# ScalarE rounds queries and keys and builds the diagonals; GpSimd keeps the low halves and splits a second output chunk early

## The chip, the cores and the metric

The program runs on 1 core of a Trainium2 chip. The metric is device time in microseconds (us) of one execution. The core has five engines that run beside each other and are tied only by semaphores: TensorE (PE in the profile: matmuls; PEld: its weight loads), VectorE (DVE), ScalarE (ACT), GpSimd (POOL) and SyncE (SP), which here only starts DMAs. Each engine runs its own instructions strictly in order, so a wait in one instruction holds up everything behind it on that engine.

## What is computed

Four layers on a 512 x 1024 fp32 stream: two layers of kind A (sliding-window attention SWA with 6 heads, a pooling mixer, causal latent attention MLA with 6 heads, then a gated MLP), one of kind R (a gated linear recurrence beside cross-attention XA with 4 heads over 256 memory rows) and one of kind F (causal "forgetting" attention FOX with 8 heads beside XA with 4), the last two with a squared-ReLU MLP.

```python
for l in range(DEPTH):                       # kind A, twice
    proj = rms_norm(x, attn_norm[l]) @ w_in[l]
    q_a, k_a, v_a, u_b, cq_c, ckv_c, kr_c = jnp.split(proj, split_idx, axis=-1)
    mixed = concat([swa_mixer(q_a, k_a, v_a, ...), pool_mixer(u_b, ...), mla_mixer(cq_c, ckv_c, ...)])
    x = x + mixed @ w_out[l]
    h = rms_norm(x, ffn_norm[l])
    x = x + (jax.nn.silu(h @ w_gate[l]) * (h @ w_up[l])) @ w_down[l]
for layer in range(DEPTH):                   # kind R, then kind F
    h = rms_norm_2(x, norm_mix[layer])
    y_mix, xq = rglru_group(h, ...) if layer == 0 else fox_group(h, ...)
    y_mem = memory_group(xq, mem, ...)       # XA: softmax(rms(q) rms(k)^T / sqrt(128)) v
    x = x + concat([y_mix, y_mem]) @ w_out[layer]
    x = x + sqrelu_mlp(rms_norm_2(x, norm_mlp[layer]), w_mlp_in[layer], w_mlp_out[layer])
```

Every attention head is softmax(q k^T) v with normalized q and k.

## The kernel before

**Precision.** TensorE works on fp32r, a rounded fp32. To keep fp32 accuracy an operand is held as a high half (the value rounded to fp32r) and a low half (the rest), and each product takes three passes: high x high, high x low, low x high (lines 807 to 816, by the helper `passes`).

**Weights.** They stream from HBM in chunks of 16 blocks of 128 x 128 (1 MB) into two slots `raw0`, `raw1`. GpSimd splits a chunk into `wh` and `wl` (`split`, lines 612 to 638): it waits until the chunk has landed, then (line 618) until TensorE has begun the chunk before it (`w_used`), which shows that the slot's old content is used up; then two TENSOR_SCALAR of 128 x 1024 (L627) and four TENSOR_TENSOR of 128 x 512 (L633). TensorE takes 48 matmuls for a chunk.

**One attention stage**, in the order of the work for head hd (units: the query tiles, of one or two heads):
- VectorE `prep` (line 1962) scales a unit's query and key tiles into `t[:, 0]`, `t[:, 1]` and signals `norm_qk`.
- GpSimd `prep` (line 709) rounds them to `qh`, `kh` (L669) and signals `hi_ready`; then forms `ql`, `kl` (L665) and signals `qk_ready`. From the third unit on it first waits until the scores of the unit before have released the slot (line 714).
- TensorE `score_rows` (line 1094): q x k of the high halves, query rows on the partitions, in two halves (two row blocks each) into banks 0 and 1. It waits for `hi_ready` at a unit's start.
- VectorE `maxima` (line 2026): TENSOR_REDUCE of the row maxima (L2034, L2041, L2043, L2045) into `mx`; for SWA also the maximum with the sink (L1651); then two TENSOR_SCALAR (L2052), one for each row block, that write -max times the identity into `dg`. After the second half `dg_ready`.
- TensorE `score_columns` (line 1124) waits for `dg_ready`, and at a unit's start for `qk_ready`; keys on the partitions: three passes, then `ones_r` x `dg` (L1150), which subtracts each query's maximum; masks or biases. Banks 2 and 3.
- ScalarE `exponentials` (line 1512) writes `pt`; TensorE `weighted` (lines 1172, 1182, 1187) multiplies with the values into bank 4; ScalarE `reciprocal` (line 1534, two activations of `rt`); VectorE `out` (line 2057) multiplies into `sq`, which has two buffers, so it first waits until GpSimd has consumed the output two before; GpSimd `mixed` (L669 and L705) rounds and splits it into `act`. `weighted` of the next head waits until bank 4 is emptied by `out`.

TensorE, VectorE, ScalarE and GpSimd each go through the heads in a fixed order: TensorE score_rows(hd+1) first half, score_columns(hd), score_rows(hd+1) second half, weighted(hd-1); VectorE maxima(hd+1) first half, prep, out(hd-2), maxima(hd+1) second half, and in layer R one step of the recurrence (`recurrence`, line 1888); ScalarE reciprocal(hd-2), exponentials(hd); GpSimd prep, at one head (`chunk_at`: 3 in SWA, 3 in XA of layer R, 5 in FOX) the split of the first of the four chunks of the output projection, then mixed(hd-2).

**Output projection.** `out_proj` (line 1222) uses the four chunks one after the other, two banks each; the first needs the mixed tiles one by one, the second waits for its split and for VectorE's `resid` (line 2102), which adds the first two banks to x (L1647, x<-x,ps). Chunks 2 to 4 of this projection are split after the attention (line 769). In layer 0 VectorE runs `decay_rates` (line 1742, about 30 instructions on 128 x 4 elements) between the last `out` and `resid`.

## Time and profile before

| | us |
|---|---|
| median of 3 runs | 2573.95 (2565.67 to 2575.25) |
| the profiled execution | 2568.36 |
| its span in the trace | 2566.6 |
| mean granted clock of TensorE | 0.964 of full speed |

| engine | busy us | share of the span | instructions |
|---|---|---|---|
| PE | 2391.1 | 93% | 10786 |
| DVE | 1204.1 | 47% | 1482 |
| ACT | 406.3 | 16% | 688 |
| POOL | 1723.7 | 67% | 1432 |

Busy time is the time in which an engine had an instruction of its own under way; the shares say who could be the limit on average, not who is the limit in a stage. The stages with attention are at 100 to 265 us (layer 0), 755 to 908 (layer 1), 1440 to 1502 (layer 2, kind R) and 2045 to 2168 (layer 3, kind F); the rest is projections and MLPs.

### The profile page before, as it was taken

How to read it: one execution, taken by the hardware profiler on the slowest of the kernel's cores; microseconds unless marked ns; L12 is line 12 of the kernel's file. 1: busy time of each engine (PE TensorE's matmuls, PEld its weight loads, DVE VectorE, ACT ScalarE, POOL GpSimd, SP SyncE). 2: the span in 40 equal slices, each digit the busy share in tenths (PEclk: the TensorE clock that was granted, in tenths of full speed). 3: DMA queues.
4: the chain of work that ended last, by engine and by line, in shares of the span. 5: the costliest groups of instructions: out<-in, count | busy, mean ns of one | idle time of the engine just before them, and what ended most of it. 6: DMA issues, size and time to landing. Idle time of an engine off the chain costs nothing. (4 is left out here: it accounts for less than half of the span.)

```text
span 2566.6 us, 29137 instructions
## 1 busy us (share of the span) xinstructions
PE 2391.1 (93%) x10786; PEld 1922.9 (75%) x10786; DVE 1204.1 (47%) x1482; ACT 406.3 (16%) x688; POOL 1723.7 (67%) x1432
## 2 busy tenths in 40 slices
PE   5978899999997899999998789999999898999999
PEld 4666688888866678888886558888887675888887
DVE  7776543332378644332248655315345463550340
ACT  3122111110122311111011411001111132110000
POOL 5565677777756577777776577767765655786774
PEclk9988999999998899999999789999999988999999
DMA  4210122223321012222232112222232200222222
GB/s 141 91 38 1 66 98 98 98 73 101 113 67 53 1 67 98 98 98 84 96 118 79 50 66 91 101 90 95 99 115 82 83 17 2 97 98 99 98 98 82
DMA packets 37841, 207.89 MB, mean 81 GB/s; under 512 B 3532, under 2 KB 10316, under 8 KB 16888
## 3 DMA queue, kind: packets, MB, share of 16 engines
q1 hardware_dynamic: 37752, 206.70, 23.2%
q8 instruction: 56, 0.92, 0.1%
q14 instruction: 33, 0.27, 0.0%
HBM read 204.55 MB, written 2.13 MB: 81 GB/s over the span
## 5 line engine op out<-in xcount | busy, mean ns | idle before, releaser
L633 POOL TENSOR_TENSOR wl<-raw,wh 128x512 fp32r<-128x512 f32 (+1 forms) x776 | 1051.8, 1387 | 0.0
L627 POOL TENSOR_SCALAR wh<-raw 128x1024 fp32r<-128x1024 f32 (+1 forms) x388 | 430.7, 1130 | 593.4 <-PE ps L811 447.7
L811 PE MATMUL ps<-h,wh 128*128 128x512 f32 x1576 | 618.6, 392 | 27.9 <-POOL wl L633 9.2
L815 PE MATMUL ps<-h,wh 128*128 128x512 f32 x1576 | 614.4, 390 | 0.0
L816 PE MATMUL ps<-h,wl 128*128 128x512 f32 x1576 | 614.4, 390 | 0.0
L811 PE MATMUL ps<-act,wh 128*128 128x512 f32 x1120 | 438.3, 391 | 7.4 <-DVE x L1647 5.6
L815 PE MATMUL ps<-act,wh 128*128 128x512 f32 x1120 | 436.5, 390 | 0.0
L816 PE MATMUL ps<-act,wl 128*128 128x512 f32 x1120 | 436.3, 390 | 0.0
L811 PEld LDWEIGHTS ps<-h,wh 128*128 128x128 f32 x1576 | 296.5, 188 | 100.1 <-issue 29.4
L816 PEld LDWEIGHTS ps<-h,wl 128*128 128x128 f32 x1576 | 296.4, 188 | 62.2
L815 PEld LDWEIGHTS ps<-h,wh 128*128 128x128 f32 x1576 | 296.7, 188 | 61.8 <-issue 1.0
L1647 DVE TENSOR_TENSOR x<-x,ps 128x512 f32<-128x512 f32 x80 | 55.0, 688 | 483.8 <-PE ps L816 483.3
L811 PEld LDWEIGHTS ps<-act,wh 128*128 128x128 f32 x1120 | 210.8, 188 | 53.4 <-issue 6.6
L816 PEld LDWEIGHTS ps<-act,wl 128*128 128x128 f32 x1120 | 210.7, 188 | 44.1
L815 PEld LDWEIGHTS ps<-act,wh 128*128 128x128 f32 x1120 | 210.8, 188 | 43.9 <-issue 0.5
L1647 DVE TENSOR_TENSOR t<-ps,rstd 128x512 f32<-128x512 f32 x108 | 74.7, 692 | 105.5 <-PE ps L816 104.4
L1647 DVE TENSOR_TENSOR nt<-ps,rstd 128x512 f32<-128x512 f32 x44 | 30.4, 692 | 192.9 <-PE ps L816 192.7
L1647 DVE TENSOR_TENSOR ssq<-ssq,sq 128x512 f32<-128x512 f32 (+1 forms) x80 | 81.0, 1013 | 78.9 <-ACT sq L1320 78.1
L1320 ACT ACTIVATE h<-x,vec 128x512 fp32r<-128x512 f32 x64 | 46.3, 724 | 449.3 <-DVE x L1647 438.5
L1320 ACT ACTIVATE act<-t 128x512 f32 (+1 forms) x64 | 40.5, 633 | 462.7 <-DVE t L1655 462.7
L1647 DVE TENSOR_TENSOR act<-t,act 128x512 f32 (+1 forms) x64 | 69.0, 1077 | 63.6 <-ACT act L1320 63.6
L669 POOL TENSOR_SCALAR qh<-t 128x512 fp32r<-128x512 f32 (+1 forms) x30 | 18.5, 617 | 119.3 <-DVEq L1994 50.5
(339 smaller groups left out, 2896.4 us busy)
## 6 DMA issues: line engine op xcount, KB each, us to landing
raw<-w_gu SPq DMA_DIRECT2D x44, 1024.0 KB, 4.8
raw<-w_up SPq DMA_DIRECT2D x32, 1024.0 KB, 4.8
raw<-w_down_b SPq DMA_DIRECT2D x32, 1024.0 KB, 4.8
raw<-w_down_a SPq DMA_DIRECT2D x32, 704.0 KB, 4.0
raw<-w_in_a SPq DMA_DIRECT2D x14, 1024.0 KB, 4.8
raw<-w_in_f SPq DMA_DIRECT2D x13, 1024.0 KB, 4.9
raw<-w_in_r SPq DMA_DIRECT2D x11, 1024.0 KB, 4.9
raw<-w_out_a SPq DMA_DIRECT2D x8, 1024.0 KB, 7.8
```

Of the source, the lines that this page charges most:

```text
L627: pool.tensor_scalar(hi_s[:, part], raw[s][:, part], 1.0, 1.0, ALU.mult, ALU.mult).then_inc(hi_done, 1)
L633: ins = pool.tensor_tensor(lo_s[:, part], raw[s][:, part], hi_s[:, part].bitcast(F32), ALU.subtract)
L669: pool.tensor_scalar(out, in0, scale, 1.0, ALU.mult, ALU.mult).then_inc(hi_done, 1)
L811: first = pe.matmul(out, w_hi, v_hi, start=start, stop=False)
L815: pe.matmul(out, w_hi, v_lo, start=False, stop=False)
L816: return pe.matmul(out, w_lo, v_hi, start=False, stop=stop)
L1320: return sc.activation(out, in_, f, **kw)
L1647: dve.tensor_tensor(out, in0, in1, op).then_inc(sig.sem, 1)
```

## The change

1. Rounding queries and keys moves from GpSimd to ScalarE: ScalarE gets a `prep` of its own, which waits for `norm_qk` (and for the slot), writes `qh` and `kh` with ACT.Copy and signals `hi_ready`. GpSimd's `prep` waits for `hi_ready` and writes only the low halves.
2. The diagonals move from VectorE to ScalarE (`diagonals`): an activation of the identity with the maximum as its scale. The sign goes into the ones (`neg_ones_r`). `mx` gets a second buffer. VectorE keeps the reduces, and for SWA the maximum with the sink, which signals `max_ready`.
3. ScalarE's order for head hd becomes reciprocal(hd-2), diagonals(hd+1) first half, exponentials(hd), prep, diagonals(hd+1) second half.
4. GpSimd splits two output chunks within the attention. The first is at SWA head 3 as before, at XA head 2 in layer R (was 3) and at FOX head 4 (was 5). The second is at MLA head 3, XA head 4 in layer R and FOX head 7; in place of `w_used` it waits for the last filling of the bank that the slot's old chunk fed (`slot_done`). After the attention two chunks are left instead of three.

```diff
+            def split(s, nblk, first=False, slot_done=None):
...
-                if not first:
+                if slot_done is not None:
+                    pool.wait_ge(ready[slot_done], bk.filled(slot_done, -1))
+                elif not first:
                     pool.wait_ge(w_used, used.at())
...
-            def prep(m, u, after=None):
-
-
-                pool.wait_ge(norm_qk, nqk.up())
-                if after is not None:
...
+            def prep(m, u):
+
+
+                pool.wait_ge(hi_ready, qkh.up())
                 s, sk = m.slot(u), m.kslot(u)
...
-                tsc(qh[s][q, :], t[q, 0, :])
-                for r, (k_hi, k_lo) in zip(parts, keys):
-                    tsc(k_hi[r, 0:n], t[r, 1, 0:n])
-                pool.sem_inc(hi_ready, 1)
                 tt(ql[s][q, :], t[q, 0, :], qh[s][q, :].bitcast(F32), ALU.subtract)
...
                     if hd == chunk_at:
 
                         split_all(1, BLOCKS)
+                    if hd == second_at:
+
+                        split_all(1, BLOCKS, slot_done)
...
-                    attention(MLA)
+                    attention(MLA, second_at=3, slot_done=7)
...
-                    attention(XA, None, 3, True)
+                    attention(XA, None, 2, True, second_at=4, slot_done=3)
...
-                    attention(FOX, XA, 5)
+                    attention(FOX, XA, 4, second_at=7, slot_done=0)
                     attention(XA)
-                split_all(n_out - 1, nblk)
+                split_all(n_out - 2, nblk)
...
+            def prep(m, u, after=None):
+
+
+                sc.wait_ge(norm_qk, nqk.up())
+                if after is not None:
+                    sc.wait_ge(ready[3], bk.filled(3, (2 * after + 1) if m.kind == "causal" else after))
+                q, n = m.qrows(), m.nkeys()
+                last = fn(qh[m.slot(u)][q, :], t[q, 0, :], ACT.Copy)
+                for r, (k_hi, k_lo) in key_parts(m, u):
+                    last = fn(k_hi[r, 0:n], t[r, 1, 0:n], ACT.Copy)
+                last.then_inc(hi_ready, 1)
...
+                    for i in (0, 1) if half == 0 else (2, 3):
+                        ins = fn(dgs[m.name][hd % 2][:, i, :], ident[:, :], ACT.Copy, scale=mx[hd % 2][:, i:i + 1])
+                    if half:
+                        ins.then_inc(dg_ready, 1)
+
+                diagonals(0, 0)
+                prep(m, 1)
+                diagonals(0, 1)
                 for hd in range(m.heads + 2):
                     if hd >= 2:
                         reciprocal(hd - 2)
+                    if hd + 1 < m.heads:
+                        diagonals(hd + 1, 0)
                     if hd < m.heads:
                         exponentials(hd)
+                    if m.starts(hd):
+                        prep(m, m.starts(hd), hd)
+                    if hd == m.heads and nxt:
+                        prep(nxt, 0)
+                    if hd + 1 < m.heads:
+                        diagonals(hd + 1, 1)
...
-                    for i in two:
-                        ins = dve.tensor_scalar(dg[:, i, :], ident[:, :], mx[:, i:i + 1], -1.0, ALU.mult, ALU.mult)
-                        if i == TB - 1:
-                            ins.then_inc(dg_ready, 1)
-                            dgr.up()
```

How it stands on the engines. GpSimd in layer 0, MLA heads 2 to 4 (`act<-sq` is mixed, `qh`, `kh`, `ql`, `kl` are prep), before:

```order
L669 TENSOR_SCALAR act<-sq 64x512
L705 TENSOR_TENSOR act<-sq,act 64x512
L669 TENSOR_SCALAR qh_79<-t 96x512
L669 TENSOR_SCALAR kh_83<-t 64x512
L665 TENSOR_TENSOR ql_81<-t,qh_79 96x512
L665 TENSOR_TENSOR kl_85<-t,kh_83 64x512
L669 TENSOR_SCALAR act<-sq 64x512
```

And now, at the same place:

```order
L722 TENSOR_TENSOR act<-sq,act 64x512
L682 TENSOR_TENSOR ql_81<-t,qh_79 96x512
L682 TENSOR_TENSOR kl_85<-t,kh_83 64x512
L644 TENSOR_SCALAR wh_54<-raw_52 128x1024 x2
L650 TENSOR_TENSOR wl_56<-raw_52,wh_54 128x512 x4
L686 TENSOR_SCALAR act<-sq 64x512
```

The two roundings are gone, and the second output chunk stands between the last prep and the mixing of MLA's second head.

GpSimd in layer R, XA heads 1 to 5, before (each `act<-sq` pair is one mixed; after the one of the recurrence at head 1 came head 2's two, then the split):

```order
L665 TENSOR_TENSOR kl_85<-t,kh_83 128x256
L669 TENSOR_SCALAR act<-sq 128x512
L705 TENSOR_TENSOR act<-sq,act 128x512
...
L627 TENSOR_SCALAR wh_55<-raw_53 128x1024 x2
L633 TENSOR_TENSOR wl_57<-raw_53,wh_55 128x512 x4
```

And now:

```order
L682 TENSOR_TENSOR kl_85<-t,kh_83 128x256
L686 TENSOR_SCALAR act<-sq 128x512
L722 TENSOR_TENSOR act<-sq,act 128x512
L644 TENSOR_SCALAR wh_55<-raw_53 128x1024 x2
L650 TENSOR_TENSOR wl_57<-raw_53,wh_55 128x512 x4
...
L644 TENSOR_SCALAR wh_54<-raw_52 128x1024 x2
L650 TENSOR_TENSOR wl_56<-raw_52,wh_54 128x512 x4
```

The first split has moved ahead of head 2's two outputs; four outputs lie between it and the second split, two behind that.

ScalarE in SWA of layer 0, from the reciprocal of one head on (`rt` reciprocal, `pt` and `es` exponentials), before:

```order
L1320 ACTIVATE rt<-es 64x512
L1320 ACTIVATE rt<-rt 64x512
L1320 ACTIVATE pt_a<-ps 128x512
L1320 ACTIVATE pt_a<-ps 128x384
L1320 ACTIVATE es<-ps,vec 64x512
```

And now:

```order
L1333 ACTIVATE rt<-es 64x512
L1333 ACTIVATE rt<-rt 64x512
L1333 ACTIVATE dg_96<-ident,sm 128x128 x2
L1333 ACTIVATE pt_a<-ps 128x512
L1333 ACTIVATE pt_a<-ps 128x384
L1333 ACTIVATE es<-ps,vec 64x512
L1333 ACTIVATE dg_96<-ident,sm 128x128 x2
```

The exponentials of a head now stand behind the first two diagonals of the next head and ahead of the last two.

## Rows read from the trace of the kernel before

**Rows 1.** Busy time by stretch: start:end length, busy us of each engine, clock, DMA.
```profile
400.00:450.00 50.00, 50.00 (x223) 41.39 (x222) 19.27 (x19) 5.72 (x9) 35.43 (x28) 1.00 0.29 105
128.00:203.00 75.00, 54.59 (x322) 45.21 (x321) 58.71 (x99) 19.43 (x33) 41.99 (x43) 0.87 0.09 34
203.00:262.00 59.00, 51.23 (x238) 38.82 (x237) 34.85 (x65) 17.82 (x36) 37.96 (x40) 0.88 0.00 1
1440.00:1502.00 62.00, 39.79 (x122) 23.59 (x122) 42.31 (x55) 9.98 (x17) 34.10 (x33) 0.72 0.07 27
```

**Rows 2.** Waits of PE over the span: waiter, awaited, us in total, times, longest.
```profile
PE ps L1187 <- DVE sq L1647: 17.8, 5, 10.0
PE ps L1120 <- POOLq L723: 13.0, 6, 4.9
PE ps L811 <- DVE x L1647: 11.6, 7, 5.6
PE ps L1146 <- DVE dg L2052: 8.1, 4, 4.1
PE ps L1182 <- DVE sq L1647: 7.9, 6, 2.5
PE ps L1104 <- POOLq L723: 7.9, 4, 3.2
PE ps L1146 <- DVE dg_swa L2052: 4.9, 5, 1.2
```

**Rows 3.** Groups by form: shapes, count, busy us, mean ns, idle before.
```profile
L2052 DVE TENSOR_SCALAR dg<-ident,sm 128x128 fp32r<-128x128 f32 x136 | 67.4, 537 | 5.3
L1320 ACT ACTIVATE pt<-ps 128x128 f32<-128x128 f32 x6 | 1.7, 277 | 1.7 <-PE ps L1152 1.7
L1320 ACT ACTIVATE pt<-ps,nck 128x128 f32<-128x128 f32 x4 | 1.5, 368 | 1.0 <-PE ps L1152 1.0
L1320 ACT ACTIVATE act<-t 128x512 f32 x48 | 30.4, 633 | 221.4 <-DVE t L1655 221.4
L669 POOL TENSOR_SCALAR qh<-t 128x512 fp32r<-128x512 f32 x18 | 11.1, 619 | 82.1 <-DVEq L1994 39.2 <-PE ps L1152 15.8 <-PE ps L1155 14.0
L705 POOL TENSOR_TENSOR act<-sq,act 64x512 fp32r<-64x512 f32 x32 | 40.7, 1271 | 2.7
```

**Rows 4.** Order of time, layer 0's output projection, DVE, then POOL, then PE.
```profile
270.25 1.21 DVE L1647 TENSOR_TENSOR sm<-sm 128x4 f32<-128x4 f32 x1
274.37 0.17 DVE L1651 TENSOR_SCALAR sm<-sm 128x4 f32<-128x4 f32 x1
278.03 0.69 DVE L1647 TENSOR_TENSOR x<-x,ps 128x512 f32<-128x512 f32 x1
...
268.89 5.02 POOL L633 TENSOR_TENSOR wl<-raw,wh 128x512 fp32r<-128x512 f32 x4
...
278.86 0.77 PE L811 MATMUL ps<-act,wh 128*128 128x512 f32 x1 [5.58 <-DVE x L1647]
```

**Rows 5.** Order of time, layer 1, SWA head 3, DVE.
```profile
817.49 2.52 DVE L2052 TENSOR_SCALAR dg<-ident,sm 128x128 fp32r<-128x128 f32 x2
```

**Rows 6.** Order of time, layer 1, MLA's last heads, ACT, DVE, POOL, PE.
```profile
885.79 0.28 ACT L1320 ACTIVATE pt_a<-ps 128x128 f32<-128x128 f32 x1 [0.31 <-PE ps L1152]
...
896.53 0.69 DVE L1647 TENSOR_TENSOR sq<-ps,rt 64x512 f32<-64x512 f32 x1 [1.92 <-issue]
...
888.83 1.29 POOL L665 TENSOR_TENSOR kl<-t,kh 64x512 fp32r<-64x512 f32 x1
...
902.81 3.84 PE L1172 MATMUL ps<-pt_a,vom 128*128 128x512 f32 x8 [2.12 <-DVE sq L1647]
```

**Rows 7.** Order of time, layer R, XA's last heads, POOL, DVE, PE.
```profile
1485.54 6.72 POOL L633 TENSOR_TENSOR wl<-raw,wh 128x512 fp32r<-128x512 f32 x4
...
1494.44 0.69 DVE L1647 TENSOR_TENSOR sq<-ps,rt 128x512 f32<-128x512 f32 x1 [4.52 <-POOL act L705]
...
1495.18 3.78 PE L1187 MATMUL ps<-pt0b,rxv 128*128 128x512 f32 x4 [9.96 <-DVE sq L1647]
```

More of the change, by code:

```diff
@@ L224, in half, with qrows, nkeys @@
         return h % 2 if self.per_unit == 2 else 0
+    def qrows(self):
+        return slice(0, 96) if self.name == "mla" else slice(0, P)
+    def nkeys(self):
+        return M_MEM if self.name == "xa" else T
     def vrow(self, h):
@@ L306, in build @@
         anti_r = keep("anti_r", [P], F32R)
-        ones_r = keep("ones_r", [P], F32R)
+        neg_ones_r = keep("neg_ones_r", [P], F32R)
         maskt_r = keep("maskt_r", [P], F32R)
@@ L337, in build, with key_parts @@
         key_tiles = {"swa": swa_k, "mla": one_k, "fox": fox_k, "xa": one_k}
+        def key_parts(m, u):
+            if m.name == "swa" and u:
+                return []
+            keys = key_tiles[m.name][m.kslot(u)]
+            rows = slice(0, 64) if m.name == "mla" else slice(0, P)
+            return zip([rows] if len(keys) < 2 else [slice(0, 64), slice(64, P)], keys)
         pt0 = view("pt0", H_AT + 16384, [4 * T])
@@ L638, in split @@
                 split_out.up()
-            nqk = Count(norm_qk, kept)
+            qkh = Count(hi_ready, kept)
             mixo = Count(mix_out, kept)
@@ L1149, in score_columns @@
                         maxima = dg[:, q0 // P:(q0 + n) // P, :].rearrange("p b n -> p (b n)")
-                        last = pe.matmul(out, ones_r[:, :], maxima, start=False, stop=m.kind == "full")
+                        last = pe.matmul(out, neg_ones_r[:, :], maxima, start=False, stop=m.kind == "full")
                         if m.kind == "causal":
@@ L1420, in in_a @@
                     fn(kraw[:, i, :], ps[tt % 4][:, :], ACT.Copy).then_inc(free[tt % 4], 1)
+                prep(SWA, 0)
                 for i in range(MLA_HEADS):
@@ L1503, in in_f @@
                 stat(6, 1, full, 2, 1.0 / D)
+                prep(FOX, 0)
                 for i in range(4):
@@ L1509, in in_f, with attention @@
                 bk.close(USES_IN_F)
-            def attention(m, l):
+            def attention(m, l, nxt=None):
                 def exponentials(hd):
@@ L1546, in reciprocal, with diagonals @@
                     fn(rt[v, :], rt[v, :], ACT.Exp, scale=-1.0).then_inc(recip_ready, 1)
+                def diagonals(hd, half):
+                    if m.name == "swa":
+                        sc.wait_ge(max_ready, mxr.up())
+                    elif m.kind == "causal":
+                        sc.wait_ge(free[0], bk.emptied(0, 2 * hd + half))
+                        sc.wait_ge(free[1], bk.emptied(1, 2 * hd + half))
+                    else:
+                        sc.wait_ge(free[half], bk.emptied(half, hd))
+                    for i in (0, 1) if half == 0 else (2, 3):
[5 more added lines that the diff above has]
+                diagonals(0, 1)
                 for hd in range(m.heads + 2):
@@ L1582, in _ @@
                     in_a()
-                    attention(SWA, l)
+                    attention(SWA, l, MLA)
                     attention(MLA, l)
@@ L1594, in _ @@
                         in_f()
-                        attention(FOX, l)
+                        attention(FOX, l, XA)
                     attention(XA, l)
@@ new lines, in maxima @@
+                        return
+                    b = half
+                    dve.wait_ge(ready[b], bk.filled(b, hd))
+                    if m.kind == "band" and b == 0:
+                        dve.tensor_reduce(mxs[:, 0:1], ps[0][:, P:256], AX_X, ALU.max).then_inc(dve_step, 1)
+                        dve.wait_ge(dve_step, chain.up())
+                        dve.tensor_reduce(mxs[:, 1:2], ps[0][:, 256:T], AX_X, ALU.max).then_inc(free[0], 1)
+                    else:
+                        dve.tensor_reduce(mxs[:, 2 * b:2 * b + 2], ps[b][:, :].rearrange("p (a c) -> p a c", a=2),
+                                          AX_X, ALU.max).then_inc(free[b], 1)
```

59 lines of the change are left out of this document (23 added, 36 removed).

## The prediction

> **What bounds the kernel now.** I read the stages first, then who waits for whom, then the order of time at the places that wait. In a stretch of the MLP TensorE is busy for all of its 50 us at full clock [rows 1]: nothing of the change lies there, and such stretches are some four fifths of the span. In the attention stretches TensorE is not full: in 128 to 203 us it works 54.6 of 75, in 203 to 262 it works 51.2 of 59, in 1440 to 1502 only 39.8 of 62, at a mean clock of 0.87, 0.88 and 0.72 [rows 1]. VectorE is the busiest of the others there (58.7 of 75), ScalarE the idlest (19.4 of 75, 10.0 of 62). So what can be won is idle time of TensorE in the attention, and of it what these waits hold [rows 2]: for the diagonals 8.1 + 4.9 us; for the output buffer `sq`, through bank 4, 7.9 us in SWA and 17.8 in XA; for `hi_ready` 7.9 + 13.0 us; and for the first add to x, 11.6, of which 5.6 once, in layer 0. These 71 us are the ceiling, apart from the clock: it is at the 1.2 GHz level in parts of these stretches.
>
> **Part 1: the diagonals leave VectorE.** The 136 instructions (two for each half of a head, 68 pairs) cost 67.4 us there, 537 ns each on average [rows 3]. A pair takes from 0.5 us up to 2.52 us, the latter while GpSimd splits a chunk [rows 5]. On ScalarE an activation of the same size takes 277 ns, with a per-partition operand 368 [rows 3]; those read PSUM, these read SBUF. I take 0.65 us a pair (bounds 0.55 and 0.8), 44 us for the 68 pairs, beside TensorE's work except at the handoffs.
> The row behind this: a VectorE instruction on 128x2 or 128x4 elements in SBUF takes 0.17 us alone and 1.21 while GpSimd is splitting [rows 4]. The Trainium skill ("SBUF — State Buffer", section "Who interferes with whom") says that the port pair which VectorE and GpSimd share is locked for a whole instruction and that ScalarE never waits for it; the trace agrees on the VectorE side, and for ScalarE no pair of such rows exists yet. By that page's rule the diagonals would cost the same beside a split.
> In SWA the chain is: VectorE reduces, out(hd-2) with ScalarE's two reciprocal steps between, reduce, diagonal; each weighted() and score_columns() waits on it, 7.9 and 4.9 us in both layers together [rows 2]. With 0.5 to 2.5 us per head off VectorE I expect the heads without a split to become TensorE-bound and the one with a split to keep about 1 us. ScalarE's chain there, reciprocal 1.26 (two of 0.633 [rows 3]), diagonals 0.65, exponentials about 1.8, diagonals 0.65, ends just about when TensorE has done weighted(hd-1). Gain: 12.8 less 5 that stays, or 8 us for the two layers. The waits of 8.1 us at the first heads (4.1 at most) shrink little, since only two pairs lie on that chain, by 0.5 each: 1 us is in the 8.
>
> **Part 2: rounding on ScalarE.** GpSimd takes 619 ns a tile [rows 3] and comes late where it is mixing outputs (a mixed is 0.62 + 1.27 us [rows 3]); ScalarE takes 633 ns for a copy of that size from SBUF [rows 3], so the move itself is neutral and the gain is the queue ahead of it. At the second unit of MLA and of both XA stages TensorE waits up to 3.2 and 4.9 us for it [rows 2]. GpSimd's mixed goes from that path, 1 us in each A layer, 1.3 in layer F, 0.5 at the start in R. Where GpSimd only waited for the slot, ScalarE has to finish the exponentials first and nothing changes; in F's second such place I count +0.3. Sum: 2 us in the A layers, 2 in F with 0.5 for the chunk and the FOX start. What hides the copies in the steady state: in MLA head 3 the last exponential ends at 886.07 [rows 6]; copies 1.24, diagonals 0.65 give 888.0, and the next score_columns starts at 888.9. The cover is 0.9 us. If it is gone, each head pays the excess.
>
> **Part 3: the second chunk early.** In the projection itself it is worth little in layers 1, R and F: the second chunk was ready 0.3 to 0.5 us after the bank that it also waits for, so 0.3 us each. Its price is 7.1 us of GpSimd time (2.1 + 5.0 [rows 4]), up to 9.4 beside a busy VectorE (2.7 + 6.7, its second part in [rows 7]). In MLA: low halves end about 890.0 (before 890.12 [rows 6]), the split 897.2, mixed(1) 899.1. VectorE's out(3), at 896.53 before [rows 6], must wait for that mixed since `sq` has two buffers: 2.6 us later, weighted(4) 1.5 us later, and with it the rest, since GpSimd has mixed(2) only at 901.1. Cost +1.5 in each A layer, and +0.25 where the diagonals delay the first exponential: 3.2 us for both, net of 0.3. At FOX head 7 GpSimd has room, no cost.
> In layer 0 it takes something else away. The split at 266.9 to 273.9 [rows 4] runs beside `decay_rates`, whose tiny instructions then take 1.2 us instead of 0.17 [rows 4]; so the add to x comes at 278.03 and TensorE stands for 5.58 us [rows 4]. With the chunk already split GpSimd is idle there: some 30 instructions at 0.2 us end before TensorE has done the first chunk, the gap falls to the 1.0 us of the add, and 4.6 us go. After that gap TensorE ran at 1.2 GHz for a while (the first matmul 0.77 us against 0.39): another 1.2. Together 5.8.
>
> **Part 4: layer R.** Before, the split sat between the recurrence step of head 2 and output 1. VectorE waited for GpSimd's mixed until 1494.44, and TensorE stood 9.96 us [rows 7]. Now the first split starts as soon as the recurrence output of head 1 is mixed, about 3 us earlier than the old order would reach that point since VectorE is 5 us of diagonals lighter: 1470 to 1479.4 at the contended 9.4. Output 0 and recurrence 2 are then mixed by 1483.3; output 1 leaves VectorE at 1482.1 (0.6 us later than now), recurrence 3 at 1487.2, output 2 at 1490.5 where it was 1495.1. The last weighted() follows at once, at half or full clock (3.8 or 2.0 us [rows 7] for its first part), and the projection starts 4.6 to 7 us earlier. The second split (1489 to 1496) makes output 2's mixed late, 1498.4, but the projection's first chunk needs it only at its seventh block, 4 us in. I take 5.5.
>
> **The sum.** 2568.4 - 8 (SWA) - 2 (A layers' rounding) + 3.2 (MLA's end) - 5.8 (layer 0's projection) - 5.5 (R) - 2 (F) = 2548.3, a change of -20 us or 0.8%. The profiled execution lies 5.6 us below the median of the three runs; the same change from the median is 2554. I give 2553.
>
> **The rivals.**
> A. As worked out, -14 to -27 us.
> B. More: the shorter gaps also keep the clock at 2.4 GHz through the starts of SWA, MLA and XA, where a stretch of layer R shows 0.72 and SWA 0.87 [rows 1]. If a third of the time lost to the low clock there (about 30 us in all, from 0.13 x 75 in one SWA, as much in the other, and 0.28 x 62 less the idle part) comes back: -30, 2543. Against it: the 5 us waits at the two starts of MLA, on VectorE, are untouched.
> C. ScalarE's order takes part of the gain: the exponentials stand behind diagonals that wait for VectorE's reduce, and VectorE stands in out() until GpSimd has mixed. If the diagonals cost 0.8 a pair and SWA keeps 1 us a head more (10 heads), with R at 4: about -8, 2566. Both splits contended at 9.4 us give the same, +2.3 at each MLA end.
> D. Slower: ScalarE becomes the bound. Place: diagonals(hd+1) second half, behind exponentials and copies, in MLA and FOX. The cover is 0.9 us where I could read it; the 12 heads of MLA, 8 of FOX and 12 of SWA would each have to exceed it by 1.1 us, +35 against -20, which gives +15 and 2589. It decides from 0.63 us a head on (20 us over 32 heads). Against it: ScalarE works 5.7 us in 50 outside and 19.4 in 75 here [rows 1], and the added 44 us + 30 units of copies fit.
> The Trainium skill ("VectorE: DVE Perf Modes", section on the TRN2 errata) speaks on D's side: a ScalarE instruction that reads SBUF pays a fixed 224 cycles, so many small ones are dear. An estimate from its figures for 128 elements at 1.2 GHz is 0.29 us each, 0.59 a pair; by it the sum would be some 1 us better than mine, and no row here shows an SBUF read of 128 columns on ScalarE.
> E. The change doesn't do what it says: the second split waits, since its chunk has not landed or the bank's count is met late. Then the projection finds it late as now, layer 0's 5.8 is lost and the A layers gain less: -12, 2562.
>
> **How the numbers follow.** A 0.45, B 0.15, C 0.22, D 0.09, E 0.09. A measurement of this kernel can tell about 0.5%, 13 us, from no change. A (but for its edge) and B are faster by more, C and E are within, D is slower: faster 0.60, same 0.31, slower 0.09. The range takes in A, C, E and most of B, with 5 us for the spread of the runs: 2535 to 2570.
>
> **What would show it.** In the new profile: the wait of L811 for the add to x has lost its 5.6; `sm` instructions of 128x4 all near 0.17; diagonals on ScalarE in pairs of 0.6 to 0.7, also during splits; the waits for diagonals in SWA near zero; in MLA's last two heads a wait for `sq` of 3 to 4 us where it was 2.1; in R no wait near 10 us, but one of about 6 before output 1. I am wrong if TensorE waits for ScalarE's diagonals in the middle of MLA or FOX (D), if a pair takes over 0.8 (C), or if the stretches 1440 on show the higher clock (B).

## The result, and the profile after

The changed kernel takes 2547.35 us (median of 4 runs, 2546.21 to 2551.81), the kernel before beside it 2574.56 (2565.67 to 2575.25). The ratio is 0.9905, 95% interval 0.9881 to 0.993: faster by about 1%. The prediction was 2553 us with a range of 2535 to 2570. The profiled execution took 2546.21 us (span 2544.4) where that of before took 2568.36. All medians and ratios below are of fast runs; one run of r_both came in a slower state, at 3440.56 us and a mean granted clock of 0.65, and is left out.

The page of the changed kernel, span and busy time of the engines. VectorE lost 76 us of work, ScalarE gained 84, GpSimd lost 36. TensorE was busy 2385.7 us where it was busy 2391.1 with the same matmuls, so of the 22.2 us by which the span is shorter 16.8 are idle time and 5.4 are a higher granted clock:

```profile
span 2544.4 us, 29116 instructions
PE 2385.7 (94%) x10786; PEld 1918.6 (75%) x10786; DVE 1128.1 (44%) x1322; ACT 490.2 (19%) x910; POOL 1687.4 (66%) x1370
```

Waits of TensorE over the span, changed kernel (waiter, awaited, us in total, times, longest), beside [rows 2]:

```profile
PE ps L1198 <- DVE sq L1699: 14.2, 5, 6.2
PE ps L1183 <- DVE sq L1699: 11.9, 5, 3.7
PE ps L1131 <- ACT kh L1333: 9.4, 4, 4.0
PE ps L1157 <- ACT dg_swa L1333: 7.2, 6, 1.9
PE ps L822 <- DVE x L1699: 7.1, 10, 1.1
PE ps L1115 <- ACT kh L1333: 4.8, 4, 1.6
PE ps L1157 <- ACT dg L1333: 4.2, 6, 1.7
PE ps L822 <- POOL act L722: 1.9, 1, 1.9
PE ps L1193 <- DVE sq L1699: 0.5, 2, 0.3
```

Line numbers have moved: L1198 was L1187 (weighted, XA), L1183 was L1172 (MLA), L1193 was L1182 (SWA), L1157 was L1146 (diagonals), L1131 and L1115 were L1120 and L1104 (rounded halves), L822 was L811. The sum of the seven lines of [rows 2] was 71.2 us; what answers to them is 47.4. MLA's end (L1183) is not among the seven: it was 5.7 before and is 11.9 now. SWA's wait for bank 4 went from 7.9 to 0.5, but its wait for the diagonals rose from 4.9 to 7.2. The 1.9 for `act` is a wait of layer R's projection, read below. The longest single waits, 10.0 in layer R and 5.6 at the first add to x, are 6.2 and 1.1 now.

Groups by form: the diagonals and the roundings on ScalarE, and one pair of diagonals in layer 0 while GpSimd splits (171.2 to 176.2), in order of time:

```profile
L1333 ACT ACTIVATE dg<-ident,sm 128x128 fp32r<-128x128 f32 x136 | 47.0, 393 | 50.3 <-DVE sm L2085 22.0 <-DVE sm L2094 16.2 <-DVE sm L2099 11.9
L1333 ACT ACTIVATE qh<-t 128x512 fp32r<-128x512 f32 x18 | 11.3, 626 | 16.7 <-DVEq L2046 16.6
...
172.20 0.70 ACT L1333 ACTIVATE dg<-ident,sm 128x128 fp32r<-128x128 f32 x2
```

One diagonal takes 393 ns, and a pair 0.69 to 0.70 us since the two overlap. A pair beside a split takes the same 0.70, where VectorE's took 2.52 [rows 5]. The 67.4 us of [rows 3] became 47.0.

**A ledger by stage.** Where the time went can be read closely, since both kernels run the same VectorE instructions in the same order at the ends of the stages. I take their start times as marks: the first reduce of a stage, SWA's sum of head 4 (es<-ps,es), MLA's out(2) and out(5), the last out of layers R and F, and the last add to x of a projection. The first column starts at the last add of layer 0's attention projection, so it holds layer 0's MLP too. An entry is how much longer or shorter a kernel takes from mark to mark than the kernel before (us, profiled executions; two values are layers 0 and 1).

| | to SWA start, layer 1 | SWA | MLA to out(2) | out(2) to out(5) | projection, layer 0 | R | projection, R | F |
|---|---|---|---|---|---|---|---|---|
| changed | +1.0 | -5.9, -5.4 | -1.9, -2.0 | +3.8, +4.1 | -7.0 | -8.2 | +3.3 | -4.4 |
| only_diag | +0.8 | -5.6, -6.2 | +2.4, -0.7 | -0.2, +0.8 | +0.8 | -6.9 | 0.0 | -5.6 |
| only_round | +1.0 | +1.3, +0.7 | -1.0, -1.0 | 0.0, +0.3 | -0.1 | -0.9 | 0.0 | -4.4 |
| undo_diag | +1.0 | +1.2, +0.7 | +1.5, -1.1 | +3.7, +3.9 | -7.0 | -3.4 | 0.0 | -3.4 |
| undo_round | 0.0 | -5.0, -4.6 | +1.5, +1.5 | +3.8, +5.1 | -7.0 | -7.0 | +3.3 | -4.3 |
| undo_second | +1.0 | -5.9, -5.5 | -2.0, -2.1 | +0.5, +0.7 | -0.1 | -6.9 | 0.0 | -1.4 |
| mla_count | +1.0 | -5.9, -5.4 | -1.9, -2.0 | +0.5, +0.8 | -7.0 | -8.2 | +3.4 | -4.5 |
| mla4 | +1.0 | -5.9, -6.3 | -2.0, -1.9 | +3.9, +4.5 | -7.0 | -6.5 | 0.0 | -4.0 |
| mla4_r4 | +1.0 | -5.9, -6.3 | -2.0, -1.9 | +0.5, +0.7 | -7.0 | -12.7 | +1.0 | -4.7 |
| r_both | -0.5 | -4.9, -6.5 | -2.0, -2.0 | -1.2, +0.7 | -6.3 | -8.2 | -0.5 | -4.0 |
| best2 | -0.8 | -4.1, -5.8 | -1.9, +0.2 | +0.5, -0.9 | -7.0 | -12.7 | 0.0 | -1.4 |
| decay_first | 0.0 | 0.0, 0.0 | 0.0, 0.0 | 0.0, +0.2 | -6.5 | -0.3 | 0.0 | -5.2 |

The rest (layer 0's start, 0.7 to 2.8 us later than in the kernel before, the MLPs, the other projections) adds 0.3 to 4.2 us. How far a single entry can be trusted is seen where the code is the same: SWA, MLA and the projections mostly repeat within 0.1 us, sometimes only within 2.5; layer R with its projection gave -4.9 and -6.5 for the same code (changed, mla4), and layer F -4.4, -4.5, -4.0, -4.7, -4.0 and -1.4 for one code, 0 and -5.2 for the other. The last is the clock, below. It has its part in other entries too: MLA to out(2) in only_diag is the same code in both layers and reads +2.4 at a mean granted clock of 0.75 (TensorE busy 46.6 us) and -0.7 at 0.84 (busy 42.0). SWA's gain in the changed kernel is free of it: TensorE is busy 40.3 and 40.2 us there where it was 39.7 and 41.2, and the idle time fell by 11.0 us in the two layers.

### The profile page after: what moved, and what is told of

Read it like the earlier page. It is cut to its first block, busy times and chain, and to the rows that moved or that the text cites. A ratio compares the mean times of both kernels' runs of the same rounds, so it can differ in the third digit from the quotient of the medians.

```text
span 2544.4 us, 29116 instructions
## 1 busy us (share of the span) xinstructions
PE 2385.7 (94%) x10786; PEld 1918.6 (75%) x10786; DVE 1128.1 (44%) x1322; ACT 490.2 (19%) x910; POOL 1687.4 (66%) x1370
## 4 chain that ended last, share of the span: by engine, by line
PE 57%; DVE 6%; POOL 2%; ACT 2%; issue 1%; DVEq 0%; POOLq 0%; ACTq 0%
PE ps L822 17%; PE ps L826 17%; PE ps L827 17%; POOL wl L650 1%; PE ps L1183 1%; PE ps L895 1%; PE ps L1157 1%; DVE nt L1707 1%; DVE uc L1707 1%; DVE nt L1699 1%; ACT rt L1333 1%; DVE t L1707 0%; POOL wh L644 0%; POOL act L722 0%; ACT nt L1333 0%
## 5 line engine op out<-in xcount | busy, mean ns | idle before, releaser
L822 PE MATMUL ps<-h,wh 128*128 128x512 f32 x1576 | 619.2, 393 | 28.1 <-POOL wl L650 9.4
L822 PE MATMUL ps<-act,wh 128*128 128x512 f32 x1120 | 437.8, 391 | 3.0 <-POOL act L722 1.9
L822 PEld LDWEIGHTS ps<-h,wh 128*128 128x128 f32 x1576 | 296.9, 188 | 100.2 <-issue 29.5
L822 PEld LDWEIGHTS ps<-act,wh 128*128 128x128 f32 x1120 | 210.7, 188 | 49.2 <-issue 3.1
L682 POOL TENSOR_TENSOR ql<-t,qh 128x512 fp32r<-128x512 f32 (+1 forms) x30 | 38.7, 1290 | 154.3 <-ACT kh L1333 75.9
```

Source lines behind the costliest of these rows:

```text
L682: pool.tensor_tensor(out, in0, in1, op).then_inc(hi_done, 1)
L822: first = pe.matmul(out, w_hi, v_hi, start=start, stop=False)
```

## The experiments

Each run was timed beside the kernel before, on the same chip, and its ratio is to that; the chips of different runs differ, so ratios compare better than medians.

### One part undone at a time: undo_diag, undo_round, undo_second

undo_diag, on VectorE in `maxima`, and the same two lines taken from ScalarE:

```diff
+                def diagonals(hd, half):
+                    for i in (0, 1) if half == 0 else (2, 3):
+                        ins = dve.tensor_scalar(dgs[m.name][hd % 2][:, i, :], ident[:, :],
+                                                mx[hd % 2][:, i:i + 1], 1.0, ALU.mult, ALU.mult)
+                    if half:
+                        ins.then_inc(dg_ready, 1)
```

> The changed kernel with the diagonals back on VectorE, directly behind its reduces (the minus stays in the ones, mx keeps its two buffers); rounding and the splits stay as changed. Theory 1, the parts act at separate places and add up: the 9.4 us that the two SWA stages gained go (the waits for the diagonals and for bank 4 come back there), about 1 us at each MLA start, and in layer R VectorE is again 5 us later at output 1, of which 2 to 3 us reach the end. Sum +12, about 2559 us. Theory 2, the SWA gain came mostly from rounding on ScalarE (GpSimd's roundings no longer stand before the mixed outputs): +3, about 2550, and the intervals between the sink sums of SWA stay at 6.0 to 7.0 us.

Measured: 2568.56 us (2564.0 to 2571.31), ratio to before 0.9984 (0.9973 to 0.9995). Without the diagonals nearly nothing of the gain is left, some 20 us less of it. That is more than either theory gave: SWA loses 7.1 and 6.1 us against the changed kernel and is slower than before, MLA's start loses 3.4 and 0.9, layer R with its projection 1.5. Theory 2 falls. Of theory 1 the places hold, the size doesn't. MLA's start in layer 0 is partly the clock: only_round, with the same code up to there, has -1.0 at a mean clock of 0.80 where undo_diag has +1.5 at 0.75.

undo_round, in GpSimd's `prep`, with ScalarE's `prep` removed:

```diff
+                pool.wait_ge(norm_qk, qkh.up())
+                if after is not None:
+                    pool.wait_ge(ready[3], bk.filled(3, (2 * after + 1) if m.kind == "causal" else after))
...
+                tsc(qh[s][q, :], t[q, 0, :])
+                for r, (k_hi, k_lo) in key_parts(m, u):
+                    tsc(k_hi[r, 0:n], t[r, 1, 0:n])
+                pool.sem_inc(hi_ready, 1)
```

> The changed kernel with the rounding back on GpSimd, ahead of its low halves; diagonals on ScalarE and the splits stay as changed. Theory 1: the second unit of MLA is late again (the wait for the rounded halves from 1.6 back to over 3 us), 2 us in each A layer; 1 to 2 us in layers R and F; MLA's end gets no better. Sum +5 to +7, about 2553 us. Theory 2, the rounding carries the SWA gain: +10 or more, about 2558, with the SWA intervals back near 8.5.

Measured: 2557.97 us (2553.93 to 2559.86), ratio 0.9934 (0.9915 to 0.9954). By the ledger the rounding is worth 3.4 us at each MLA start (-1.9 to +1.5, and -2.0 to +1.5), 0.8 to 0.9 in each SWA, and it costs 1.0 before each SWA. Of the 3.4 us 1.1 is idle time of TensorE (8.9 us for 7.9); the other 2.3 are the same matmuls at a mean clock of 0.75 for 0.80, and whether that comes with the change isn't shown. The SWA gain stays (theory 2 falls).

undo_second, four calls back to their old form:

```diff
-                    attention(MLA, second_at=3, slot_done=7)
+                    attention(MLA)
...
-                    attention(XA, None, 2, True, second_at=4, slot_done=3)
+                    attention(XA, None, 3, True)
...
-                    attention(FOX, XA, 4, second_at=7, slot_done=0)
+                    attention(FOX, XA, 5)
...
-                split_all(n_out - 2, nblk)
+                split_all(n_out - 1, nblk)
```

> The changed kernel with the splits as in the kernel before: one chunk early, at SWA head 3, XA head 3 and FOX head 5, none second. Theory 1: MLA's end loses its price, 3.8 us earlier in each A layer (7.6); layer 0's projection stands again for 5 to 6 us before the first add to x, and the starts of the projection's later chunks give back 1.5; layer R is back at its long wait before output 1, +4; layer F +1 to 2. Sum +4 to +6, about 2552 us. Theory 2, the second split costs more than it brings: below 2547.

Measured: 2549.21 us (2547.57 to 2551.11), ratio 0.9906 (0.9888 to 0.9925), against 0.9905 for the changed kernel. The entries come as theory 1 had them in the A layers: 3.3 us a layer back at MLA's end, 6.9 lost in layer 0's projection. Layer R with its projection is at -6.9 where the changed kernel is at -4.9, so moving the splits there brought nothing that shows. The early second chunk as a whole is worth nothing that can be measured: the ratios are equal, each within some 5 us.

### One part alone: only_diag, only_round

Both are the edits above put together: only_diag is undo_round with undo_second, only_round is undo_diag with undo_second.

> The kernel before with the diagonals alone on ScalarE (sign in the ones, mx with two buffers, ScalarE's order as changed); rounding on GpSimd and the splits as before. Theory 1, the diagonals carry nearly all: SWA 5 us earlier in each A layer, MLA's start 1.5 us later than before (its unit 1 still waits for GpSimd), layer R 5 to 7 us earlier, layer F 1 to 2: -12 to -14, about 2555 us where the kernel before has about 2568. Theory 2, the parts only work together: within 5 us of the kernel before.

> The kernel before with the rounding alone on ScalarE (GpSimd keeps the low halves); diagonals on VectorE and the splits as before. Theory 1: alone it gives nothing: 1 us lost at each SWA start (ScalarE rounds ahead of the squares that VectorE waits for), about 1 in each SWA, 0 to 1 won at the MLA starts: 0 to +4 us against the kernel before. Theory 2, as the prediction had it: 2 us won in the A layers and 1 to 2 elsewhere, -3.

Measured: only_diag 2549.79 us (2548.32 to 2553.35), ratio 0.9917 (0.99 to 0.9934); only_round 2567.26 (2565.11 to 2571.63), ratio 0.999 (0.9978 to 1.0002). The diagonals alone give nearly the whole gain, the rounding alone none that can be told from zero. Waits of TensorE in only_round:

```profile
PE ps L1193 <- DVE sq L1679: 7.3, 4, 2.4
PE ps L1115 <- ACT kh L1333: 6.3, 4, 2.5
```

With the diagonals on VectorE, SWA's wait for bank 4 is still there (7.3; 7.9 before), whoever rounds.

The two parts add up. By the whole times it is 0.83% for the diagonals and 0.10% for the rounding alone, and 0.94% for both (undo_second). At the MLA start the ledger seems to say otherwise (+2.4 and -0.7 for the diagonals, -1.0 twice for the rounding, -2.0 and -2.1 for both), but that is mostly the clock, as said above. The wait of TensorE for the second unit's rounded halves in layer 0 is read without it: 3.18 us before, 2.50 with the diagonals alone on ScalarE, 2.28 with the rounding alone, 1.64 with both. The kernel before, then the changed kernel:

```profile
211.00 0.47 PE L1104 MATMUL ps<-kh,qh 128*128 128x128 f32 x1 [3.18 <-POOLq L723]
204.82 0.48 PE L1115 MATMUL ps<-kh,qh 128*128 128x128 f32 x1 [1.64 <-ACT kh L1333]
```

The 1.0 us that rounding costs ahead of SWA can be read in the changed kernel, layer 0, order of time: ScalarE rounds the first unit before it takes the first square of the latent queries, and VectorE waits for that square. Before, the same instruction waited 1.17 us; in both layers the wait is 2.60 to 2.63 in every kernel traced that rounds there and 1.15 to 1.17 in every other one.

```profile
121.06 0.63 ACT L1333 ACTIVATE qh<-t 128x512 fp32r<-128x512 f32 x1 [2.25 <-DVEq L2046]
121.60 0.61 ACT L1333 ACTIVATE kh<-t 64x512 fp32r<-64x512 f32 x1
122.22 0.63 ACT L1333 ACTIVATE khb_swa<-t 64x512 fp32r<-64x512 f32 x1
122.87 0.59 ACT L1333 ACTIVATE sq<-ps 96x512 f32<-96x512 f32 x1
...
123.60 0.69 DVE L1699 TENSOR_TENSOR qc<-ps,cgq 96x512 f32<-96x512 f32 x1 [2.63 <-ACT sq L1333]
```

### MLA's end: mla_count, mla4

The changed kernel, layer 0, order of time: VectorE's out(3) and out(4) (sq<-ps,rt), GpSimd's mixing (act<-sq a head, act<-up a pooled tile), TensorE's weighted of heads 4 and 5:

```profile
248.24 0.69 DVE L1699 TENSOR_TENSOR sq<-ps,rt 64x512 f32<-64x512 f32 x1 [5.43 <-POOL act L722]
248.99 2.42 PE L1183 MATMUL ps<-pt,vom 128*128 128x512 f32 x8 [1.49 <-DVE sq L1699]
252.99 1.26 POOL L722 TENSOR_TENSOR act<-up,act 128x512 fp32r<-128x512 f32 x1
254.38 0.68 DVE L1699 TENSOR_TENSOR sq<-ps,rt 64x512 f32<-64x512 f32 x1 [5.44 <-POOL act L722]
255.12 4.12 PE L1183 MATMUL ps<-pt_a,vom 128*128 128x512 f32 x8 [3.70 <-DVE sq L1699]
```

out(4) starts right behind the pooled tile (252.99 + 1.26 = 254.25), not behind mixed(2), which is all that its buffer needs. VectorE's count of the mixed outputs is raised by two for the pooled tiles before out(4), though GpSimd mixes them after head 3. In the kernel before it cost nothing: out(4) at 257.50 was released by the reciprocal, the pooled tile was done at 256.90.

```diff
-                    if m.name == "mla" and hd == m.heads:
-
-                        mixs.n += 2
                     if hd >= 2:
                         out(hd - 2)
+                    if m.name == "mla" and hd == m.heads + 1:
+
+                        mixs.n += 2
```

> The changed kernel with one bookkeeping line of VectorE moved: the two pooled outputs that GpSimd mixes between MLA's outputs 3 and 4 are counted behind out(5) instead of before out(4), so that out(4) waits for mixed(2) and no longer also for the first pooled tile. Theory 1: in the changed kernel out(4) at 254.38 was released by the pooled tile at 254.25 while its reciprocal was there at 252.71; it now goes 1.5 to 1.7 us earlier in both A layers, about 3 us in all, 2544 us; the 1.5 us wait before it (out(3) for mixed(1), behind the split) stays. Theory 2, the chain through mixed(2) and the reciprocal ends at the same time: no change, 2547.

Measured: 2540.88 us (2539.44 to 2550.41), ratio 0.9885 (0.986 to 0.9911). The profiled executions differ by 6.8 us in all, twice what I expected. The same stretch in mla_count:

```profile
248.14 0.69 DVE L1699 TENSOR_TENSOR sq<-ps,rt 64x512 f32<-64x512 f32 x1 [5.43 <-POOL act L722]
252.69 0.68 DVE L1699 TENSOR_TENSOR sq<-ps,rt 64x512 f32<-64x512 f32 x1 [3.86 <-ACT rt L1333]
253.43 2.42 PE L1183 MATMUL ps<-pt_a,vom 128*128 128x512 f32 x8 [2.12 <-DVE sq L1699]
257.24 0.69 DVE L1699 TENSOR_TENSOR sq<-ps,rt 64x512 f32<-64x512 f32 x1 [3.86 <-ACT rt L1333]
```

out(4) comes 1.7 us earlier, as expected, and the eight matmuls behind it take 2.42 us instead of 4.12, which is another 1.7: they ran at full clock and not at half. The whole times alone don't tell mla_count from the changed kernel (their intervals overlap); this stretch does.

The shorter gap (2.12 us for 3.70) is not enough to explain the clock. The same eight matmuls behind the same gap of 2.12 us took 3.84 in layer 1 of the kernel before [rows 6], 4.12 in its layer 0, 4.08 and 4.06 in undo_second, 4.07 twice in mla4_r4, but 2.42 in layer 0 of r_both and in layer 1 of best2. Layer 0 of mla4_r4 and of r_both, with the same code up to there:

```profile
252.48 4.07 PE L1185 MATMUL ps<-pt_a,vom 128*128 128x512 f32 x8 [2.12 <-DVE sq L1701]
254.53 2.42 PE L1185 MATMUL ps<-pt_a,vom 128*128 128x512 f32 x8 [2.12 <-DVE sq L1701]
```

From out(2) to out(5) the mean clock is 0.91 in layer 0 of the kernel before, 0.92 in the changed kernel and 1.00 in mla_count. So the changed kernel's 3.8 us are not the clock; mla_count won 1.7 by it. Why the level differs isn't shown.

mla4 has `second_at=4` in place of 3 in MLA and the old count:

> The changed kernel with the second split of MLA one head later, behind mixed(1) instead of ahead of it; VectorE's count stays as it is. Theory 1, two waits in series: out(3) no longer waits for GpSimd (1.5 us at weighted of head 4), but GpSimd does the same work before the first pooled tile, which ends as before, and out(4) goes by the count for that tile; so MLA's end stays within 0.5 us of the changed kernel's and the total at 2547. Theory 2, only the split ahead of mixed(1) matters: MLA's end 1.5 us or more earlier in each A layer, 2544 or less.

Measured: 2550.11 us (2546.62 to 2552.07), ratio 0.993 (0.9913 to 0.9946); MLA's end +3.9 and +4.5, as in the changed kernel. Theory 1 holds: where the split stands does not matter while the count holds out(4) back. With both edits (mla4_r4, below) it is +0.5 and +0.7, as with the count alone, but not at the same clock: mla_count has full clock at the last eight matmuls of both layers, mla4_r4 half. Where both waits are gone and the clock is full, MLA's end reads -1.2 (r_both, layer 0: 16.8 us from out(2) to out(5), where mla_count takes 18.5) and -0.9 (best2, layer 1). So at equal clock the count costs about 1.6 us a layer (out(4) follows out(3) after 6.14 us, 4.55 without it) and the wait of out(3) behind the split, 1.49 us at TensorE, about 1.7.

### Layer 0's projection: decay_first

The kernel before with `decay_rates` called behind the wait for `vec` at the program's start, and ScalarE's part of it there too:

```diff
             dve.wait_ge(ld_vec, 16)
+            decay_rates()
             dve.wait_ge(ld_x, 16)
...
-                    if l == 0:
-                        decay_rates()
```

> The kernel before with the 30 small instructions of the decay rates moved to the program's start, into the time in which VectorE waits for x; nothing else changed. Theory 1: they alone, stretched by the split, made TensorE stand 5.6 us at the first add to x of layer 0; so that gap falls to the 0.7 us or less that the split itself leaves (the second chunk was split by 273.9, TensorE's first chunk ended at 273.3), -4.7 to -5.3 us, 2569. Theory 2: the add or the clock is late for another reason, and less than 2 us go.

Measured: 2558.92 us (2555.43 to 2567.92), ratio 0.9979 (0.9964 to 0.9993). Order of time in layer 0's projection:

```profile
274.40 0.69 DVE L1646 TENSOR_TENSOR x<-x,ps 128x512 f32<-128x512 f32 x1 [7.48 <-PE ps L816]
...
275.69 0.50 PE L811 MATMUL ps<-act,wh 128*128 128x512 f32 x1 [0.72 <-POOL wl L633]
```

The gap of 5.58 us [rows 4] is 0.72. The ledger has -6.5 here: 5.3 up to the first add to x and 1.2 from there to the last, in which TensorE ran at a mean clock of 1.00 instead of 0.94. Theory 1 holds, with nothing but the small instructions moved. In the changed kernel GpSimd is idle there, nearly all of the instructions take 0.16 to 0.17 us, and the add comes when TensorE has finished:

```profile
264.39 0.16 DVE L1699 TENSOR_TENSOR sm<-sm 128x4 f32<-128x4 f32 x1
269.56 0.69 DVE L1699 TENSOR_TENSOR x<-x,ps 128x512 f32<-128x512 f32 x1 [0.54 <-PE ps L827]
...
270.39 0.47 PE L822 MATMUL ps<-act,wh 128*128 128x512 f32 x1 [0.26 <-DVE x L1699]
```

### Layer R: mla4_r4, r_both, best2

The changed kernel, layer R, order of time: the first split (1456.77 to 1466.4), VectorE's out(1) behind the mixing that stood behind it, weighted(2); then the projection's first wait for a mixed tile behind the second split:

```profile
1456.77 2.91 POOL L644 TENSOR_SCALAR wh<-raw 128x1024 fp32r<-128x1024 f32 x2 [0.22 <-POOL act L722]
...
1459.65 6.74 POOL L650 TENSOR_TENSOR wl<-raw,wh 128x512 fp32r<-128x512 f32 x4
...
1468.57 0.69 DVE L1699 TENSOR_TENSOR sq<-ps,rt 128x512 f32<-128x512 f32 x1 [4.52 <-POOL act L722]
...
1469.32 3.78 PE L1198 MATMUL ps<-pt,rxv 128*128 128x512 f32 x4 [6.21 <-DVE sq L1699]
...
1487.19 0.61 PE L822 MATMUL ps<-act,wh 128*128 128x512 f32 x1 [1.90 <-POOL act L722]
```

mla4_r4 has both edits of MLA, and in layer R the first split ahead of GpSimd's prep of unit 1:

```diff
+                if chunk_at == -1:
+                    split_all(1, BLOCKS)
                 prep(m, 1)
...
-                    attention(XA, None, 2, True, second_at=4, slot_done=3)
+                    attention(XA, None, -1, True, second_at=4, slot_done=3)
```

> Three edits on the changed kernel in two stages that can be read apart. MLA: split one head later and the count moved. Theory: with both waits gone MLA's end comes as early as without a second split, so the step from mid MLA to its end is +0.5 where the count alone gave +0.5 too (then the head of the split is worth nothing more) or, if both count, -0.5 to 0. Layer R: the first split moved ahead of GpSimd's prep of unit 1, where GpSimd was idle from 1427.7 to 1435.1; the second stays at head 4. Theory R1: alone in that gap it takes 7.1 us instead of 9.6, and TensorE's 6.2 us wait before weighted(2) (out(1) behind the split) goes: the end of XA 5 us earlier, while the 3.8 us that layer R gives back before its first add to x stay. Theory R2: without that split VectorE becomes the bound in the same place (recurrence 9 us an output): 2 us or less. Total by theory 2547.4 - 6.6 - 5, about 2536.

Measured: 2534.82 us (2533.35 to 2537.04), ratio 0.987 (0.9854 to 0.9887). The interval overlaps the changed kernel's (from 0.9881) by a little and is clear of mla4's (from 0.9913), which ran beside it. The split and weighted(2) in mla4_r4:

```profile
1420.40 2.06 POOL L644 TENSOR_SCALAR wh<-raw 128x1024 fp32r<-128x1024 f32 x2 [0.32 <-POOL kl L682]
1422.43 4.99 POOL L650 TENSOR_TENSOR wl<-raw,wh 128x512 fp32r<-128x512 f32 x4
...
1457.06 1.98 PE L1200 MATMUL ps<-pt,rxv 128*128 128x512 f32 x4 [0.41 <-DVE sq L1701]
```

The split takes 7.0 us instead of 9.6, in time that GpSimd had free, and the wait of 6.21 is 0.41. Layer R is 12.7 us shorter than before where the changed kernel is 8.2 shorter and mla4, with the same code as it there, 6.5. Theory R1 holds, except that the projection gives back 1.0 us and not the 3.8 that it expected to stay.

r_both differs by `second_at=2`:

> As mla4_r4, but the second split of layer R at head 2 (where the changed kernel has the first) instead of head 4. Theory R1: the 3.8 us before the first add to x go, since no split stands ahead of the last two mixed outputs, but the split beside VectorE's recurrence comes back with its wait of up to 6 us before output 1: against mla4_r4 the end of XA is 5 us later and the add 1 us later. Theory R2: the wait before output 1 is smaller than in the changed kernel since GpSimd has fewer outputs queued: the add 2 to 4 us earlier than in mla4_r4.

Measured: 2535.32 us (2534.01 to 2543.55), ratio 0.9883 (0.9853 to 0.9913). As theory R1 has it: layer R is back at -8.2 with a wait of 6.2, and its projection gives back nothing.

best2 has no second split in layer R and rounds SWA's unit 0 behind the first square of the latent queries:

```diff
-                prep(SWA, 0)
                 for i in range(MLA_HEADS):
+                    if i == 1:
+                        prep(SWA, 0)
```

> The changed kernel with the MLA split at head 4, the count behind out(5), ScalarE's rounding of SWA's unit 0 behind the first square of the latent queries instead of ahead of it, and in layer R the first split ahead of unit 1's prep and no second one; FOX as changed. Theory: against mla4_r4 the 1.0 us at each SWA start goes (2 us), and layer R gives back nothing before its first add to x (1.5 us); 2531 us. Rival: GpSimd's windows start later behind the later rounding and SWA's unit 1 is late for it: no gain at the SWA starts, 2533 or more.

Measured: 2533.96 us (2528.84 to 2535.8), ratio 0.9847 (0.983 to 0.9865), the best of all with mla4_r4, from which it can't be told. Layer R's projection gives back nothing (0.0 for +1.0), and SWA starts 1.8 us earlier in layer 1; but MLA's start there is at +0.2 where it was -1.9, so up to out(5) that layer is only 0.8 us shorter than in mla4_r4. The loss at MLA's start is the clock: TensorE is busy 44.0 us there for 42.0, and idle 9.4 for 9.2. Its place is read in the trace, but in the whole time the later rounding brings nothing that can be measured.

### The clock in layer F

Layer F's attention as one window (length, busy time, mean granted clock as the third number from the end). The kernel before, then decay_first, whose code in layer F is the same:

```profile
2054.77:2169.80 115.03, 100.56 (x425) 72.75 (x426) 57.50 (x117) 36.08 (x64) 57.31 (x62) 0.86 0.03 10
```

```profile
2050.93:2160.77 109.84, 94.53 (x425) 68.94 (x426) 57.40 (x118) 36.06 (x64) 57.45 (x62) 0.91 0.03 10
```

The changed kernel, then best2, whose code in layer F is the changed kernel's:

```profile
2037.58:2148.17 110.59, 96.60 (x425) 70.89 (x426) 39.98 (x69) 60.07 (x129) 54.27 (x51) 0.89 0.06 20
```

```profile
2023.86:2137.51 113.65, 98.97 (x425) 71.23 (x426) 39.99 (x70) 60.09 (x129) 54.38 (x51) 0.86 0.06 19
```

The same 425 matmuls took 94.5 or 100.6 us, by the clock that was granted. The lengths of the two codes overlap (109.8 and 115.0 against 110.6 and 113.7). So the 4.4 us that the ledger shows for layer F are no proof of a gain there. TensorE's idle time in the window is 14.5 and 15.3 us with the old code, 14.0 and 14.7 with the new, so only some 0.5 us of the 4.4 can be put down to the code. The spread between executions of one kernel goes with the clock as well: runs of mla_count took 2539.44 us at a mean of 0.971 and 2550.41 at 0.967, runs of decay_first 2555.43 at 0.968 and 2567.92 at 0.962.

## Why the prediction was right

The time fell in the range, 6 us under the point, and the main mechanism was the one named. By the ledger of the two profiled executions (-22.2 us; the sum forecast -20.1) some terms were wrong and cancelled, and 5.4 of the 22.2 are the clock, which only the term of layer 0's projection had counted on. That the time came so near the point is in part luck.

- **Diagonals, cost.** 0.65 us a pair was taken, 0.69 measured; the same beside a split (0.70). The Trainium skill ("SBUF — State Buffer", section "Who interferes with whom") says that ScalarE never waits for the port pair of VectorE and GpSimd; now there is a row for it, and the trace agrees. The estimate by the Trainium skill ("VectorE: DVE Perf Modes", section on the TRN2 errata), 0.29 us an instruction and 0.59 a pair, was low: one took 393 ns, and the two overlapped.
- **SWA: -8 forecast, -11.3 measured.** The mechanism was half right. The wait for bank 4 went as said (7.9 to 0.5), the wait for the diagonals did not go near zero but rose to 7.2. At head 1 of each layer (1.94 and 1.93 us) ScalarE builds the last two diagonals behind the exponentials of the head before, as C had it. At the other four waits (0.56 and 1.1 us) ScalarE itself had stood 0.8 to 0.9 us for VectorE's maximum with the sink, an instruction on 128x2 elements that took 1.26 us beside the split where it takes 0.23. VectorE, ScalarE and TensorE of the changed kernel, layer 0:

```profile
167.74 1.26 DVE L2099 TENSOR_SCALAR sm<-sm,vec 128x2 f32<-128x2 f32 x1
169.03 0.69 ACT L1333 ACTIVATE dg_swa<-ident,sm 128x128 fp32r<-128x128 f32 x2 [0.80 <-DVE sm L2099]
169.78 0.39 PE L1157 MATMUL ps<-qh,khb_swa 128*128 128x256 f32 x1 [0.56 <-ACT dg_swa L1333]
```

"Keeps about 1 us" for one head in six was the mis-sized term, in the cautious direction: from the sink sum of the head with the split to the next it is 6.1 us where it was 9.7, no longer than for other heads.
- **Rounding in the A layers: -2 forecast, -3.9 measured at the MLA starts, where the diagonals and the clock have their part, and +2 not foreseen.** The 2 us are 1.0 before each SWA, where ScalarE rounds ahead of a square that VectorE waits for. I had costed the move as neutral but for GpSimd's queue, and had not named what is queued behind it on ScalarE.
- **MLA's end: +3.2 forecast, +7.9 measured.** This is the step that failed. "2.6 us later, weighted(4) 1.5 us later, and with it the rest" named the right wait (1.49 us measured) and followed it through the buffer rule alone. Behind it came another, out(4) on a pooled tile, through a count that the code held too high; mla_count shows 1.6 us a layer for it. The other 1.7 that mla_count gained is a higher clock than the kernel before had there. Out(3) itself came 3.2 us later behind out(2), 2.6 forecast, and out(4) another 0.6.
- **Layer 0's projection: -5.8 forecast, -7.0 measured**, the first add to x 5.3 earlier (4.6 forecast), from there to the last add 1.7 shorter, at the higher clock (1.2). decay_first shows that the small instructions beside the split were the cause. Layer 1's projection gave 0.5 for 0.3.
- **Layer R: -5.5 forecast, -4.9 measured.** The split took 9.6 us (9.4 forecast) and TensorE waited 6.2 (about 6). But "the projection's first chunk needs it only 4 us in" was wrong: it waited 1.90 us for a mixed tile behind the second split, and its window ran at 0.96 instead of 1.00, together 3.3 us given back. mla4 has the same code there and a clock of 1.00: nothing given back, and -6.5 in all.
- **Layer F: -2 forecast, -4.4 seen**, of which about 0.5 is idle time and the rest the clock.
- **The rivals.** B (clock, -30) did not come as such: the windows of [rows 1] at the same times read 0.82 and 0.90 for 0.87 and 0.88 in the A layer. Only layer R rose (0.72 to 0.86 at the same times, 0.71 to 0.83 from mark to mark), which was B's sign; TensorE's busy time fell by 1.9 us there. C needed diagonals of 0.8 a pair. D did not show: no wait for diagonals exceeds 2 us, and ScalarE is busy 31.4 of 75 us. E did not show: the second split was early in all layers.

What the sum hid is where the gain lies. The diagonals alone give 0.83% of the 0.95% in ratio, the rounding 0.10% alone, 0.11% on top of the diagonals and 0.29% on top of the other two parts, none of it clear of the noise, and the early second chunk nothing: what it won in layer 0's projection it lost at MLA's two ends.

## What to carry to other kernels

When work moves to another engine, look at what stands in line there as well: the rounding shortened a wait at the MLA starts, but on ScalarE it stood ahead of a square that VectorE needs, and what is left of the gain is not clear of the noise. Before a stage's time is put down to a change, compare the busy time of the same matmuls: if it differs, that part is the clock. When a new item is put into a queue, check every count that other engines keep of that queue; a wait one step too strict is free until the queue gets longer. And a split beside VectorE's work costs both sides (9.6 us for 7.0, 1.21 us for 0.17), so put it where GpSimd is idle and VectorE has little to do, here at the start of layer R, before asking which head can bear it.

## What the runs showed of the hardware

- VectorE instructions on 128x4 elements took about 1.2 us beside a GpSimd split and 0.16 to 0.17 without one; ScalarE's 128x128 from SBUF took 0.70 us a pair either way.
- Behind the same gap of 2.12 us the same eight matmuls took 2.42 us (full clock) in both layers of mla_count and 4.06 and 4.08 (half) in those of undo_second, so the length of the gap alone does not tell the level.
- A split of a chunk on GpSimd took 7.0 us alone and 9.6 beside a busy VectorE.
- The same code of layer F ran at a mean granted clock of 0.86 or 0.91, 115.0 or 109.8 us, in two executions.
